# A Strassen step in place of plain gate and up products in the second feed-forward stage

## The reference

```
g = h @ w_ffn_gate_2            # 1024 x 2816
v = h @ w_ffn_up_2              # 1024 x 2816
y = (silu(g) * v) @ w_ffn_down_2
x = x + post-norm(y) * a modulation
```

## Time and profile before

| | us |
|---|---|
| Median of 3 runs (2915.92 to 2917.64) | 2917.61 |
| The profiled execution, its own time | 2917.04 |
| Its span, first to last instruction | 2915.0 |
| PE busy in the span | 2821.4 (97%), 13586 matmuls |
| DVE, ACT, POOL busy | 1552.5 (53%), 797.9 (27%), 1096.8 (38%) |
| Mean granted clock | 0.991 of full speed |

### The profile page before, as it was taken

How to read it: one execution, slowest core, us unless ns; L and a number is a source line. 1 busy time by engine, 2 the same in 40 slices (tenths; PEclk the granted TensorE clock), 3 DMA queues, 4 the chain that set the end, 5 groups by cost and what they waited for, 6 DMA issues and landing times.

```text
span 2915.0 us, 37148 instructions
## 1 busy us (share of the span) xinstructions
PE 2821.4 (97%) x13586; PEld 2264.4 (78%) x13586; DVE 1552.5 (53%) x2148; ACT 797.9 (27%) x1560; POOL 1096.8 (38%) x634
## 2 busy tenths in 40 slices
PE   7999999899999999999999999999999999999998
PEld 5677777677788888888788887777787888888887
DVE  6555577738566555656844302485365443344346
ACT  4444444434111111112413113564242000000002
POOL 3555411355333233335533343222464233233334
PEclk9999999999999999999999999999999999999999
DMA  3322222032111111112321232213422111111113
GB/s 134 97 80 84 83 80 66 22 123 84 54 51 43 50 50 44 49 50 73 142 96 44 79 137 102 80 62 115 157 93 65 51 50 43 50 50 45 48 58 109
DMA packets 63817, 218.39 MB, mean 75 GB/s; under 512 B 6847, under 2 KB 10208, under 8 KB 63332
## 3 DMA queue, kind: packets, MB, share of 16 engines
q1 hardware_dynamic: 48176, 171.99, 18.1%
q10 hardware_dynamic: 15540, 45.02, 4.4%
HBM read 194.68 MB, written 19.68 MB: 74 GB/s over the span
## 4 chain that ended last, share of the span: by engine, by line
PE 86%; DVE 9%; ACT 2%; issue 2%; DMA 1%; POOL 0%; POOLq 0%; DVEq 0%; ACTq 0%; SPq 0%
PE ps L589 25%; PE ps L591 25%; PE ps L590 25%; PE ps L675 2%; PE ps L695 2%; PE ps L709 1%; PE ps L1107 1%; PE ps L1119 1%; DVE ps L2096 1%; DVE dsm L2221 1%; PE ps L712 1%; DVE ps L2079 1%; DVE arena L2239 1%; DVE ps L2120 1%; DVE arena L2183 1%
## 5 line engine op out<-in xcount | busy, mean ns | idle before, releaser
L529 POOL CAST wh<-raw 128x1024 fp32r<-128x1024 f32 x272 | 290.0, 1066 | 1637.1 <-PE ps L591 1613.1
L589 PE MATMUL ps<-hh,wh 128*128 128x512 f32 x1968 | 795.5, 404 | 10.7 <-DVE hl L2040 4.2
L591 PE MATMUL ps<-hh,wl 128*128 128x512 f32 x1968 | 770.2, 391 | 0.0
L590 PE MATMUL ps<-hl,wh 128*128 128x512 f32 x1968 | 769.8, 391 | 0.0
L531 POOL TENSOR_TENSOR wl<-raw,wh 128x1024 fp32r<-128x1024 f32 x272 | 655.7, 2411 | 21.8
L589 PEld LDWEIGHTS ps<-hh,wh 128*128 128x128 f32 x1968 | 371.7, 189 | 97.7 <-issue 17.4
L591 PEld LDWEIGHTS ps<-hh,wl 128*128 128x128 f32 x1968 | 371.0, 189 | 79.7
L590 PEld LDWEIGHTS ps<-hl,wh 128*128 128x128 f32 x1968 | 372.0, 189 | 73.1 <-issue 3.1
L2299 DVE TENSOR_TENSOR hlf<-ps,hlf 128x512 f32<-128x512 f32 x288 | 196.1, 692 | 321.7 <-PE ps L591 321.7
L589 PE MATMUL ps<-ah,wh 128*128 128x512 f32 x832 | 327.4, 394 | 5.6 <-DVE al L2111 3.1
L590 PE MATMUL ps<-al,wh 128*128 128x512 f32 x832 | 324.3, 390 | 0.0
(11 more groups left out here) (274 smaller groups left out, 3023.1 us busy)
## 6 DMA issues: line engine op xcount, KB each, us to landing
raw<-weights SPq DMA_DIRECT2D x272, 512.0 KB, 3.2
arena<-w_ada SPq DMA_DIRECT2D x48, 512.0 KB, 3.8
arena<-gate_scratch ACTq DMA_DIRECT2D x20, 512.0 KB, 5.3
arena<-x_t ACTq DMA_DIRECT2D x1, 4096.0 KB, 14.6
gate_scratch<-arena ACTq DMA_DIRECT2D x16, 256.0 KB, 2.1
x_scratch<-arena ACTq DMA_DIRECT2D x1, 4096.0 KB, 12.8
gate_scratch<-hhf ACTq DMA_DIRECT2D x16, 256.0 KB, 2.0
hhf<-x_scratch ACTq DMA_DIRECT2D x1, 4096.0 KB, 15.2
```

What stands on the lines that cost most here:

```text
L529: pool.tensor_copy(wh[:, s], raw[:, r]).then_inc(Z.wt_hi, 1)
L589: pe.matmul(out, wh[:, slot, w], xh, start=start, stop=False)
L590: pe.matmul(out, wh[:, slot, w], xl, start=False, stop=False)
L591: return pe.matmul(out, wl[:, slot, w], xh, start=False, stop=stop)
```

## The change

Sixteen tiles (4 to 19) leave the loop's scheme. For one tile, gate and value chunk side by side are a 2 x 2 block matrix of weights (two halves of the inner product by gate and value), and the activation is a 2 x 2 block matrix as well (two halves of the inner product by two halves of the tokens). Plain multiplication takes 8 block products of 12 matmuls (4 slices of 128 by 3). The new `st_up` takes 7, in Winograd's form of Strassen's algorithm, with these parts around it:

- Once: four sums of activation blocks (`x_sums`, 32 GpSimd operations of 128x512), each with its high part (ACT, `x_high`, 16 operations) and low part (GpSimd, `x_low`, 16). They need room: `hhf` (the residual x) is written to DRAM by ACT's queue and read back later by SP's, and half of the first activation blocks, overwritten by high parts, likewise (`A21`).
- For every tile: four differences of weight blocks and seven casts and subtractions of half chunks on GpSimd, and two more for the down chunk (`st_split`). Slots are handed over by half chunks, six of them.
- For every tile after the products: one copy on ACT and five additions on DVE with operands in PSUM; then two silus, two products, and two high and low parts, all by halves. The product stays in PSUM, and one pair of buffers (`GATED[1]`) serves every tile.
- `st_down` is the same 16 outputs as before. `st_step` on DVE makes the additions and both products first, then the 16 sums, then the low parts.

What counts a chunk now counts units: nine a tile (7 products, 2 halves of the down chunk) instead of three.

The core of the diff (the same mechanism's waits in head and tail, and SyncE's loads, are cut):

```diff
+            def x_sums(phase):
+                for i in range(4):
+                    ...
+                    dst, p, q, op = ((s1, *a[1][1], ALU.add), (s3, *a[1][0], ALU.add), (s1, s1, s3, ALU.add), (s2, *a[0][0], ALU.add),
+                                     (s3, s2, s3, ALU.subtract), (s2, s1, s2, ALU.subtract), (s4, *a[0][1], ALU.add),
+                                     (s4, s4, s2, ALU.subtract))[phase]
+                    ...
+                    pool.tensor_tensor(dst, p, q, op).then_inc(R.x_sum, 1)
+            split_chunks(C_WO + SL, C_FFN2 + 10)
+            for c, phases in ((10, (0, 1, 2)), (11, (3, 4)), (12, ()), (13, (5, 6)), (14, (7,))):
+                for phase in phases:
+                    x_sums(phase)
+                split_chunk(C_FFN2 + c)
+            x_low(2)
+            def st_split(n, u, between=None):
+                ...
+                arrived(0)
+                part(0, b11, 1)
+                arrived(1)
+                weight_add(b11, b12, b11, 1, 1)
+                weight_add(b12, b22, b12, 1, 2)
+                ...
+                part(1, b12, 4)
+                weight_add(weight_sum[:], b22, b11, 2, 4)
+                if between:
+                    between(1)
+                part(2, weight_sum[:], 6)
+                part(3, b21, 7)
+                if between:
+                    between(0)
+                weight_add(b21, b21, weight_sum[:], 4, 7)
+                part(4, b11, 9)
+                part(5, b21, 10)
+                if between:
+                    between(3)
+                part(6, b22, 11)
+                arrived(2)
+                part(7, raw[:, g, LO], 12)
+                part(8, raw[:, g, HI], 13)
+            st_split(0, 0, x_low)
...
+                    pe.wait_ge(Z.g_lin, n * 2 + ST_DONE)
+                    block_product(0, 0, A_BLOCK[0, 0], True)
+                    pe.wait_ge(Z.f_prod, n * 2 + ST_DONE)
+                    sums_ready(2)
+                    block_product(1, 3, S_BLOCK[2], True)
+                    pe.wait_ge(Z.a_lo, n * 2 + ST_DONE)
+                    sums_ready(1)
+                    block_product(2, 1, S_BLOCK[1], True)
+                    pe.wait_ge(R.copied, n + (2 * KT + 1))
+                    block_product(3, 0, A_BLOCK[0, 1], False)
+                    sums_ready(0)
+                    block_product(4, 2, S_BLOCK[0], True)
+                    pe.wait_ge(R.c_sum, n * 5 + (KT + 2))
+                    block_product(5, 3, A_BLOCK[1, 1], False)
+                    sums_ready(3)
+                    pe.wait_ge(R.c_sum, n * 5 + (KT + 3))
+                    block_product(6, 2, S_BLOCK[3], False)
+                def st_down(n, u):
+                    for o in range(16):
+                        ...
+                        pe.wait_ge(Z.dn_free, n * 16 + (16 * (ST_FIRST - 1) + 16 * ND + o + 1))
...
+            silu2(2)
+            high2(2)
+            x_high(2)
+            silu2(3)
+            act.wait_ge(Z.chunk_done, ffn_gate(C_FFN2, 3) + 2)
+            act.wait_ge(R.a21_out, 48)
+            x_high(1)
+            x_high(0)
+            act.wait_ge(Z.chunk_done, C_ST)
+            x_high(3)
+            high2(3)
...
+            def st_step(n):
+                ...
+                dve.wait_ge(R.copied, n + (2 * KT + 1))
+                add(ST_SUM, bank(1), ST_COPY, 2, 0)
+                add(ST_SUM7, bank(3), ST_SUM, 2, 1)
+                add(bank(1), bank(2), ST_SUM7, 4, 2)
+                add(bank(3), bank(3), ST_SUM, 5, 0)
+                add(bank(2), bank(2), ST_SUM, 6, 3)
+                ...
+                dve.tensor_tensor(bank(2), bank(2), ST_GATE[:, LO], ALU.mult).then_inc(Z.f_prod, 1)
+                dve.tensor_tensor(bank(1), bank(1), ST_GATE[:, HI], ALU.mult).then_inc(Z.f_prod, 1)
+                for o in range(16):
+                    ...
+                    dve.tensor_tensor(t, bank(4 + o % 4), t, ALU.add).then_inc(Z.dn_free, 1)
+                for half, b in ((0, 2), (1, 1)):
+                    ...
+                    dve.tensor_tensor(lo[:, half_of(half)], bank(b), hi[:, half_of(half)].bitcast(F32), ALU.subtract).then_inc(Z.a_lo, 1)
...
+                if n == 0:
+                    sp.wait_ge(Z.chunk_done, st_unit(last, 6))
+                    for i in range(2):
+                        sp.dma_start(A21[i], A21_DRAM[i]).then_inc(R.a21_in, 16)
+                elif n in (2, 3):
+                    dram, x2 = x2_half(n - 2)
+                    sp.dma_start(x2, dram).then_inc((R.x2_in0, R.x2_in1)[n - 2], 16)
```

More of the change, by code:

```diff
@@ new lines, in _ @@
+            st_split(0, 0, x_low)
+            st_split(1, 1)
+            with pool.Fori(0, (ST_N - 2) // 2) as i:
+                for u in range(2):
+                    st_split(i * 2 + (2 + u), u)
+            for c in range(tail_at(C_FFN2), N_CHUNKS):
+                n = (c - tail_at(C_FFN2)) + 13 * ST_N + C_ST
+                pool.wait_ge(Z.chunk_done, counted(c) - SL + 1)
+                pool.wait_ge((Z.raw0, Z.raw1)[c % RAW], 16 * (c // RAW + 1))
+                pool.sem_inc(Z.pace, 1)
+                pool.tensor_copy(wh[:, c % SL], raw[:, c % RAW]).then_inc(Z.wt_hi, 1)
+                pool.wait_ge(Z.wt_hi, n + 1)
+                pool.tensor_tensor(wl[:, c % SL], raw[:, c % RAW], wh[:, c % SL].bitcast(F32), ALU.subtract).then_inc(Z.split_done, 1)
@@ new lines, in st_down @@
+                def st_down(n, u):
+                    for o in range(16):
+                        f, half = o % KT, o // KT
+                        if o in (0, 4):
+                            pe.wait_ge(Z.split_done, st_unit(n, ST_BLOCKS + o // 4))
+                        pe.wait_ge(Z.dn_free, n * 16 + (16 * (ST_FIRST - 1) + 16 * ND + o + 1))
+                        slot, at_half = st_slot(u, ST_BLOCKS + f // 4)
+                        last = product(bank(4 + o % 4), slot, 4 * at_half + f % 4, GATED[1][0][:, half_of(half)],
+                                       GATED[1][1][:, half_of(half)], True, True)
+                        last.then_inc(Z.chunk_done if o in (11, 15) else Z.dn_done, 1)
@@ L1962, in _ @@
                 unit_high(2, u)
+                if u == 2:
+                    act.wait_ge(Z.n_lo, 64)
+                    for i in range(2):
+                        act.dma_start(A21_DRAM[i], A21[i]).then_inc(R.a21_out, 16)
             act.wait_ge(Z.h_hi, 12)
@@ L1965, in _, with silu2 @@
             act.sem_inc(Z.a_hi, 2)
[L1967 to L1977, removed]
+            def silu2(j):
+                act.wait_ge(Z.chunk_done, ffn_gate(C_FFN2, j) + 1)
+                act.wait_ge(Z.f_prod, j + (NL - 1))
+                act.activation(CG[j % 2], bank(0, 2), ACT.Silu).then_inc(Z.g_lin, 1)
@@ L1979, in store @@
+            with act.Fori(0, ST_N) as i:
+                st_step(i)
             def store(half, first, end):
@@ L2688, in tail2_post @@
+            with dve.Fori(0, ST_N) as i:
+                st_step(i)
             def tail2_post(half, first, end):
```

225 lines of the change are left out of this document (201 added, 24 removed).

## The result

The changed kernel takes 2887.82 us (median of 4 runs, 2886.29 to 2888.84), the kernel before on the same chip 2917.62 us (4 runs, 2915.92 to 2917.76): ratio 0.9899, 95% interval 0.9887 to 0.9911, so 30 us faster. Forecast were 2885.5 us and the range 2873 to 2904. The profiled execution took 2887.16 us, its span is 2885.4.

A forecast was written before the change was run, and what follows sets the result against it. The prediction took PE's matmul issue to bound the kernel: 2917.0 - 43.5 (matmuls) + 6.4 (DVE) + 4.0 (head) + 1.0 (tail) = 2884.9 us, 2885.5 as median. Range 2873 to 2904.

The forecast's parts named there:

- The matmuls, -43.5: Loop: 12 matmuls fewer in each of 16 tiles, 192 at 0.2267 us each, save 43.5 us.
- DVE's order, +6.4: Each loop tile: addition and two products before the first down sum delay output 4, 0.4 us a tile, 6.4 us.
- DVE's queue decides: Rival, loop: DVE waits cost 0.2 us or more each, outputs 4 to 7 stall 1.0 us a tile; 2895 us, 13%.
- GpSimd's price: Loop and head: two-input operations of 512 elements cost 1.29 us, casts 0.6; 23.3 us a tile, under 29.9.
- the contended price: Rival, head and loop: GpSimd at its contended price costs 37 us in the head, 13 in the tiles; 2924 us, 6%.
- any overlap as a lock: Rival, loop: any GpSimd and DVE overlap locks, 40 us a tile, 118 us slower, 3036 us; chance 1%.
- The head, +4.0: First Strassen tile: PE waits 0.3 us at the fifth product, 3.4 at the seventh, 0.3 for a low part; 4.0 us.
- the 0.3 for tile 3's low part: Head: PE waits 0.3 us for tile 3's low part, which ACT now makes behind four copies.
- Two of my own signs: Loop: clock stays 1.00; the forecast is wrong if block-product matmuls stand further apart than 0.227 us.
- A lock: DVE operations with two SBUF inputs contend with GpSimd: no extra time in the loop, a microsecond each in the head.
- The tail, +1.0: Tail: chunk tail+4 lands at 48 to 49, split by 51.5 to 52.5, wanted at 51.7; 1.0 us, bounds 0 and 8.
- The sum: Whole kernel: 2917.0 - 43.5 + 6.4 + 4.0 + 1.0 = 2884.9 us, median 2885.5; forecast's own chance 60%.

The follow-up runs named there:

- e3: Changed kernel with the fifth block product of each of the 16 tiles issued twice; 2925.70 us, ratio 1.0036 to the kernel before.
- e1: Changed kernel with DVE's two products per Strassen tile moved behind down sums 1 and 8; 2879.80 us, ratio 0.9874 to the kernel before.
- e5: Changed kernel with one more 128x512 DVE addition, read by nobody, ahead of the two products in each Strassen tile; 2896.90 us, ratio 0.9932 to the kernel before.
- e2: Changed kernel with the fourth block sum's four low parts made by DVE ahead of its Strassen loop, not GpSimd; 2882.96 us, ratio 0.9888 to the kernel before.
- e7: Changed kernel with four of the first Strassen tile's nine weight casts made by ACT, not GpSimd; 2885.86 us, ratio 0.9898 to the kernel before.
- e8: Kernel e6 with tile 4's TensorE wait for tile 3's low part moved from the third to the seventh product; 2875.42 us, ratio 0.9864 to the kernel before.
- e4: Changed kernel with the gate-value product written to SBUF, so low parts have two SBUF inputs; 2888.65 us, ratio 0.9904 to the kernel before.
- e6: Changed kernel with both e1's moved DVE products and e7's four casts on ACT; 2876.19 us, ratio 0.9859 to the kernel before.

## Why the prediction was right, and where its terms were off

**The matmuls, -43.5.** Right, shown by e3: distance 33.14 with twelve more, 29.92 without a stall in e1.

**DVE's order, +6.4: measured 7.5 (e1).** Right in place (output 4, once a tile, then nothing) and mechanism (e1, e5). The working gave 0.28 us a tile and I took 0.4; it is 0.48, and two steps make the difference. I let the addition start 0.04 after the last block matmul's end; it starts at 2415.50, 0.12 after 2414.99 + 0.39. I let the product start 0.03 after the addition's end; it starts at 2416.33, 0.13 after 2415.50 + 0.70. The wait and register instructions, which I had bounded by 0 and 0.15, cost 0.1 there and nothing at the next ones (0.61 and 0.60 between starts). The rival "DVE's queue decides", 1.0 a tile, falls.

**GpSimd's price.** 1.29 us forecast, 1288 ns measured (128x512, two inputs), cast 0.6 against 612 ns. The rivals with the contended price and with any overlap as a lock fall: GpSimd is busy 327 of 450 us and TensorE never waits for it in later tiles.

**The head, +4.0: measured 6.9.** The waits came where they were forecast, 0.54 for 0.3 and 3.06 (3.2 in starts) for 3.4; the 0.3 for tile 3's low part did not come. Part 6 ended at 2318.45, forecast was 2319.4, and two errors cancel in that: the sums stand 1.25 us apart where I had 1.22, over 1 us for 48 of them, but began at 2219.58 and not at 2221.2, since the stretch ahead ran 1.6 us earlier in this run:

```profile
2219.58 10.46 POOL L666 TENSOR_TENSOR hhf<-ah,al 128x512 f32<-128x512 f32 x8
2230.00 5.02 POOL L666 TENSOR_TENSOR hhf<-hhf 128x512 f32<-128x512 f32 x4
```

What the term lacked is the clock behind the wait, 2.9 us. I had priced a wait at its length. Runs e2, e3, e7 and e8, with the wait shorter or gone, have no such stretch. Two of my own signs were not met here: the clock was not 1.00 through the loop, and the seventh block product's matmuls in tile 4 stood 0.43 us apart and not 0.227. The block products of the other tiles did stand at 0.227, and their price held.

**A lock.** The rule held in both directions: DVE operations with a PSUM input kept 681 to 700 ns, and e4 and e2 show what two SBUF inputs cost. So the engines do not meet at semaphores alone, as the section on the core has it. (Where the prediction calls the case in which any overlap locks the second-slowest, it is by its own sums the slowest, 3036 us.) In the head it held GpSimd for 1 us twice (four operations in 6.02 and 6.03 us in place of 5.02), as the sums had it. One place I left out: the same DVE line as in the earlier trace rows, L2417 now, falls beside the block sums and takes 1.68 us where it took 0.91, and a matmul waits for the copies behind it:

```profile
2224.72 1.68 DVE L2417 TENSOR_TENSOR gated<-arena,gated 128x512 fp32r<-128x512 f32 x1
```
```profile
2227.40 0.50 PE L765 MATMUL ps<-gated,wh 128*128 128x512 f32 x1 [0.60 <-DVE hlf L2440]
```

That matmul starts 0.99 after the one before and the next 0.34 later, 0.9 lost where the kernel before lost 0.1. These 0.8 us are in the -0.77 ahead of the loop, under the run's earlier beginning of 1.6.

**The tail, +1.0: measured 0.23.** No matmul of the tail waits for a split; TensorE's two waits there, 1.5 and 1.0 us, are those of the kernel before, and what the 0.23 is stays open. The reads landed sooner than I had it. GpSimd's cast of chunk tail+4 (against the earlier trace rows):

```profile
2805.06 1.04 POOL L749 CAST wh<-raw 128x1024 fp32r<-128x1024 f32 x1 [4.09 <-DMA raw<-weights]
2806.18 2.39 POOL L751 TENSOR_TENSOR wl<-raw,wh 128x1024 fp32r<-128x1024 f32 x1
```

It waited 4.09 us for its weights and still ended at 2808.57; PE wants it at 2791.41 + 21.7 = 2813.1. I had the landing at 18 to 19 us into the tail, it came before 13.7: the reads of 2 MB took 11.7 us with others beside them, and while they ran the window's slices show 380 to 414 GB/s, where my 3.4 us a MB from the earlier trace rows is 308.

**The sum.** -43.5 + 7.5 + 6.9 + 0.2, with 0.8 for the lock and -1.6 for the earlier start, is -29.7, against -29.6 between the spans; the forecast had -32.1. Of the terms the clock's 2.9 is the largest that was missing; DVE's order (+1.1) and the lock (+0.8) against the tail (-0.8) and the earlier start (-1.6) cancel within 0.5. The earlier start is no effect of the change: 1.5 us of it are there at 557 us already, long before anything is changed, and it is less than what that stretch varies between runs. So the losses, 14.5 us where the forecast had 10.4 for DVE and the head, were further off than the 2.3 us between forecast and median show, and that closeness is in part luck.

## What to carry over

When the bounding engine's work falls by 12 of 144 instructions, ask for each of its waits which operation is between the last input and the first thing freed, and put the side work behind that; here an order of two products was worth 7.5 us (e1). Work that moves off a late GpSimd should not become a DVE operation with two SBUF inputs beside it: four casts (2.8 us of GpSimd's time by the expectation) on ACT gave 4.9 us, four subtractions (5.0 us) on DVE 3.8 and a grown wait. And don't price a wait of TensorE at its length alone: 3.06 us idle cost 2.9 more at half clock in the changed kernel, and less in e4.

## What the runs showed of the hardware that I had not expected

- TensorE's clock behind a wait in a loop that otherwise has none: after idle times of 3.06 (the changed kernel, e4, e5), 3.07 (e1) and 2.70 us (e6) the granted clock read 0.50 in the windows of 1 us behind, and matmuls stood 0.43 apart; after 2.34 (e2) and 0.87 us (e8) it stayed at 1.00. The change of pace came at once in the changed kernel, and 0.8 us after the restart in e6 (starts at 2309.41, 2309.64, 2309.87, 2310.26, 2310.69), and the slow stretch lasted twelve distances in the one and seven in the other.
- The length of the wait does not decide it alone. Ahead of the loop the same eight matmuls (64x512) come after the same idle time in all ten traces; in e4 the clock read 0.50 from 558 to 560 us and they took 3.36 us, in the changed kernel it read 1.00 there and they took 1.77, as in the eight others:

```profile
557.02 1.77 PE L851 MATMUL ps<-arena 64*128 64x512 f32 x8 [2.21 <-ACT arena L1710]
```
```profile
557.38 3.36 PE L851 MATMUL ps<-arena 64*128 64x512 f32 x8 [2.22 <-ACT arena L1710]
```

- A DVE operation with two SBUF inputs beside GpSimd's back-to-back subtractions can be held for more than one of them: 4.86 us in place of 1.25 (128x1024), so for about three.
- Wait instructions between dependent DVE operations cost 0.1 us in the one place where they really wait (the product starts 0.13 after the addition's end, the added operation of e5, with one wait, 0.04), and none where the value is there.
